# Second input projection of a two-layer encoder: the last third of the tokens is met from unit 6 on

## The reference

```python
x = x + rms_norm(y, g_post)              # end of layer 0, y = output projection
h = rms_norm(x, g_pre)                   # layer 1
q, k, v, gate = jnp.split(h @ w_in, SPLIT_C, axis=-1)   # 1024, 256, 256, 1024 columns
q = rms_norm(q.reshape(B, T, C_HEADS, 64), q_norm)      # per head, then rotary positions; k alike
# attention, then (o * silu(gate)) @ w_out, post-norm, residual
```

## Time and profile before

| | us |
|---|---|
| median of 3 runs | 2140.35 (2137.98 to 2148.28) |
| the profiled execution's own time | 2140.14 |
| its span, first to last instruction | 2138.4 |
| TensorE busy | 2045.5 (96%) |
| VectorE, ScalarE, GpSimd busy | 1291.7, 1125.5, 946.4 |
| mean granted TensorE clock | 0.984 |

### The profile page before, as it was taken

The page is one execution under the profiler, slowest core; times in us unless marked ns, Lnnn a source line. Parts: engine busy times, 40 slices in busy tenths (PEclk is TensorE's granted clock), DMA queues, the critical chain, the costliest instruction groups (busy, mean ns, idle before and its releaser), DMA issues.

```text
span 2138.4 us, 25149 instructions
## 1 busy us (share of the span) xinstructions
PE 2045.5 (96%) x9332; PEld 1629.6 (76%) x9332; DVE 1291.7 (60%) x1928; ACT 1125.5 (53%) x1427; POOL 946.4 (44%) x472
## 2 busy tenths in 40 slices
PE   7999998999999999999997999999999999998995
PEld 6878876788888877767785777888777777775784
DVE  6232135326777766784567777424588778888444
ACT  7142234336666666674355344243677777777331
POOL 1222234335555555565001666432566667666200
PEclk9999999999999999999998999999999999999998
DMA  5133468526665545354335233261333333333434
GB/s 187 42 130 132 148 241 321 148 80 145 133 128 114 110 109 121 86 171 157 93 114 183 83 110 108 89 199 55 76 82 74 70 66 72 80 112 99 158 94 148
DMA packets 167530, 260.29 MB, mean 122 GB/s; under 512 B 75552, under 2 KB 84384, under 8 KB 167408
## 3 DMA queue, kind: packets, MB, share of 16 engines
q1 hardware_dynamic: 167408, 258.68, 42.3%
HBM read 160.72 MB, written 97.91 MB: 121 GB/s over the span
## 4 chain that ended last, share of the span: by engine, by line
PE 82%; DVE 10%; ACT 3%; DMA 3%; issue 2%; POOL 0%; SPq 0%; DVEq 0%; ACTq 0%
PE SA L1813 11%; PE OP L1857 9%; PE SA L473 6%; PE OP L473 5%; PE SM L1739 5%; PE OP L998 5%; PE SA L998 4%; PE OP L1864 4%; PE SA L1912 4%; PE SM L1912 4%; PE OS L473 3%; PE OS L1857 2%; PE OS L998 2%; PE SM L1735 2%; PE OS L1912 2%
## 5 line engine op out<-in xcount | busy, mean ns | idle before, releaser
L2228 POOL TENSOR_TENSOR c_PL<-c_PF,c_PH 128x1024 fp32r<-128x1024 f32 x128 | 308.8, 2417 | 152.2 <-ACT c_PH L1981 81.1
L2228 POOL TENSOR_TENSOR ab_PL<-ab_PF,ab_PH 128x1024 fp32r<-128x1024 f32 (+3 forms) x128 | 266.5, 2085 | 188.9 <-ACT ab_PH L1981 130.8
L1978 ACT ACTIVATE ab_PF<-SA 128x1024 f32<-128x1024 f32 (+3 forms) x160 | 143.6, 897 | 158.0 <-PE SA L1774 83.2
L2056 DVE TENSOR_REDUCE c_MH<-SM 128x1 f32<-128x512 f32 x256 | 171.9, 687 | 75.5 <-PE SM L1739 74.8
L1978 ACT ACTIVATE c_PF<-SA 128x1024 f32<-128x1024 f32 x160 | 164.0, 1025 | 95.3 <-PE SA L1813 95.0
L394 POOL TENSOR_TENSOR e_wl<-e_raw,e_wh 128x1024 fp32r<-128x1024 f32 (+1 forms) x31 | 73.6, 2375 | 218.9 <-ACT e_wh L539 218.9
L1981 ACT ACTIVATE c_PH<-c_PF 128x1024 fp32r<-128x1024 f32 x128 | 135.7, 1061 | 4.1
L1813 PE MATMUL SA<-c_Q,c_KA 128*128 128x512 f32 x320 | 129.6, 405 | 6.4 <-ACT c_PF L1978 6.4
L1739 PE MATMUL SM<-c_KA,c_Q 128*128 128x512 f32 x320 | 127.0, 398 | 4.5 <-DVE c_MH L2056 3.0
L1813 PE MATMUL SA<-c_Q,c_KB 72*128 72x512 f32 x320 | 128.7, 402 | 0.0
L1981 ACT ACTIVATE ab_PH<-ab_PF 128x1024 fp32r<-128x1024 f32 (+3 forms) x128 | 119.6, 935 | 4.0
(11 more groups left out here) (471 smaller groups left out, 5998.3 us busy)
## 6 DMA issues: line engine op xcount, KB each, us to landing
c_Q<-qC_hi SPq DMA_DIRECT2D x32, 384.0 KB, 4.9
e_raw<-in_w_tiles SPq DMA_DIRECT2D x20, 512.0 KB, 4.2
n_raw<-in_w_tiles SPq DMA_DIRECT2D x18, 512.0 KB, 3.8
e_XF<-in_xT SPq DMA_DIRECT2D x12, 512.0 KB, 10.7
silu_gate<-e_ta SPq DMA_DIRECT2D x24, 256.0 KB, 2.0
ab_Q<-qA_hi SPq DMA_DIRECT2D x16, 384.0 KB, 5.3
ab_G<-silu_gate SPq DMA_DIRECT2D x24, 256.0 KB, 3.2
ab_res<-in_xT SPq DMA_DIRECT2D x24, 256.0 KB, 2.9
```

The lines of the kernel that those rows point to most:

```text
L1978: nc.scalar.activation(used(PF[p], h, s), used(SA, h, s), ACT.Exp).then_inc(e_done, 1)
L2056: nc.vector.reduce_max(dst, src, axis=AX_X).then_inc(m_done, 1)
L2228: nc.gpsimd.tensor_tensor(used(PL[p], h, s), used(PF[p], h, s), used(PH[p], h, s).bitcast(F32), ALU.subtract).then_inc(p_lo[0], 1)
```

## The change

`U` is reordered. Units 0 to 3 are gate tiles 0 and 1 in the first two thirds; units 4, 5, 6 are q tile 0 in thirds 2, 0, 1, so that the last third (1) is first met in unit 6; the other q and k tiles follow (to unit 33), the values are units 34 to 39. Gate tiles 0 and 1 in the last third are units 40 and 41, and as their weights are gone by then, both tiles are loaded and split a second time (`W` has 24 entries instead of 22). Gate tiles 2 to 7 keep units 42 to 59. `EARLY = 4` gates come first, in place of 6.

With it: weight tiles 2 and 3 are loaded in period 3 and split in it, by ScalarE at t = 4 and 7 and by GpSimd; units 0 and 1 are evicted in it, ahead of the last two low parts; the seven sums of squares go behind units 1, 2 and 3 in three parts; the sum over partitions and `root` of the last third come with unit 6; the first tables are prepared behind unit 3; units 4, 5 and 6 wait for the stores of gates 0 and 3, 1, 2.

```diff
-        ("values", u, 2, 512) for u in range(4)] + [("x", 12 + t, 8, D) for t in range(6)]
-    U = [(tiles[t], t, c) for c in ORDER for t in range(2)]
-    U += [(tiles[t], t, c) for t in range(2, 12) for c in range(NC)]
+        ("values", u, 2, 512) for u in range(4)] + [("x", 10 + t, 8, D) for t in range(8)]
+    EARLY = 4
+    U = [(tiles[t], t, c) for c in ORDER[0:2] for t in range(2)]
+    U += [(tiles[2], 2, c) for c in ORDER] + [(tiles[t], t, c) for t in range(3, 12) for c in range(NC)]
     U += [(("value", i), V0 + 3, i) for i in range(TT // 2)]
-    U += [(late_gates[t], V0 + 4 + t, c) for t in range(6) for c in range(NC)]
+    U += [(tiles[t], V0 + 4 + t, ORDER[2]) for t in range(2)]
+    U += [(late_gates[t], V0 + 6 + t, c) for t in range(6) for c in range(NC)]
...
-        if (period, t) == (3, 0):
-            load(sp, 2)
+        if (period, t) in ((3, 0), (3, 1)):
+            load(sp, 2 + t)
...
-                if 0 < w < len(W) - 2:
+                if 1 < w < len(W) - 2:
                     load(sp, w + 2)
...
     def gpsimd_ahead(pool):
-        for w in range(2):
+        for w in range(4):
             low_weights(pool, w)
...
-        for g in range(3):
+        for g in range(EARLY):
             gated(g)
-        low_weights(pool, 2)
-        for g in range(3, 6):
-            gated(g)
-        for n in range(6, N):
+        for n in range(EARLY, N):
             for w in splits[n]:
-                low_weights(pool, w)
+                if w > 3:
+                    low_weights(pool, w)
...
             pe.wait_ge(x_sum[c], KT - 1)
+            if c == 2:
+                pe.wait_ge(q_log, 1)
             square_sum(c, ssum[c][:])
...
-            if i < 2:
-                pe.wait_ge(deviation, NC)
+            if i < 3:
+                pe.wait_ge(deviation, i + 1)
...
-            if n in (0, 2, 4):
-                x_square_sum(n // 2)
+            if n in (0, 2, 6):
+                x_square_sum(min(n // 2, 2))
...
+            if t in (4, 7):
+                high_weights(act, 2 + t // 7)
...
-        for g in range(3):
+        for g in range(EARLY):
             sigmoid(g)
-        high_weights(act, 2)
-        root(act, 2)
-        for g in range(3, 6):
-            sigmoid(g)
-        for n in range(6, N):
+        for n in range(EARLY, N):
             for w in splits[n]:
-                high_weights(act, w)
+                if w > 3:
+                    high_weights(act, w)
+            if n == 6:
+                root(act, 2)
...
+        if qk.index(n) < 3:
+            dve.wait_ge(g_stored[s], 32 if s == 0 else 16)
...
             if t == KT + 1:
+                for n in range(2):
+                    evict(dve, n)
                 low_x(dve, 2, 6)
                 low_x(dve, 2, 7)
...
-            evict(n)
-            if n == 2:
-                for k in range(1, KT):
+            if n > 1:
+                evict(dve, n)
+            if n in (1, 2, 3):
+                for k in range(1, KT)[3 * (n - 1):3 * n]:
                     add_square(dve, 2, k)
...
-            if n in (4, 8):
-                prepare(n // 2 - 2)
+            if n in (3, 8):
+                prepare(n // 4)
```

More of the change, by code:

```diff
@@ L1223, in low_x, with evict @@
                                        ).then_inc(x_lo[j], 1)
+    def evict(dve, n):
+        c = U[n][2]
+        if kind[n] == "value":
+            dve.wait_ge(tok_done, 1)
+            dve.wait_ge(hi_done, len(qk) + 2 * (n - v0) + 2)
+            for i in range(2):
+                half, t = slice(i * 256, i * 256 + 256), 2 * (n - v0) + i
+                done = nc.vector.scalar_tensor_tensor(
+                    out=sl[stage_of(n)][:, half].bitcast(F32R), in0=bank(n)[:, half], scalar=rtok[:, t:t + 1],
+                    in1=sh[stage_of(n)][:, half], op0=ALU.mult, op1=ALU.subtract)
+            done.then_inc(acc_read, 1)
+            return
+        dve.wait_ge(mm_done, n + 1)
+        dve.wait_ge(rstd_ready, ORDER.index(c) + 1)
+        if n in gates:
+            g = gates.index(n)
+            if EARLY <= g < EARLY + 3:
+                dve.wait_ge(lo_done, len(qk))
+            wait_count(dve, g_stored[g % 3], 16 * (g // 3))
+            nc.vector.tensor_tensor(ta[g % 3][:], bank(n), rstd[:, cols(c)], ALU.mult).then_inc(acc_read, 1)
+            return
+        s = qk.index(n) % 3
+        if qk.index(n) < 3:
+            dve.wait_ge(g_stored[s], 32 if s == 0 else 16)
+        wait_count(dve, lo_done, qk.index(n) - 2)
+        nc.vector.tensor_tensor(ta[s][:], bank(n), rstd[:, cols(c)], ALU.mult).then_inc(acc_read, 1)
+        dve.wait_ge(acc_read, n + 1)
+        nc.vector.stream_shuffle(tb[s][:], ta[s][:], SWAP16).then_inc(r_swap, 1)
     def vector_ahead(dve, period, t):
@@ L1258, in prepare @@
                                         ALU.mult, ALU.mult).then_inc(tab_done, 1)
[L1260 to L1288, removed]
         def finish(n):
@@ L1307, in low @@
                                     ).then_inc(lo_done, 1)
-        dve.wait_ge(x_sum[1], KT - 1)
         for n in range(N):
```

## The result

The changed kernel takes 2152.41 us (median of 16 runs) where the kernel before, on the same chip, took 2142.2 (median of 16). The ratio is 1.0044, with a 95% interval of 1.0036 to 1.0053: 9.4 us slower. That is a slowing clear of the spread of the runs, and at the edge of the 0.5% that the prediction counts as "no change". The forecast was 2146.7 in a range from 2139.5 to 2153, so the median lies 0.6 us inside the upper end. One of the 16 runs of the changed kernel was slow (3851.26 us at a granted clock of 0.874) and is left out of the ratio; the median of the other 15 is 2152.06. The profiled execution took 2151.08 us (span 2149.3), 10.9 more in span than before. The busy shares, against the earlier trace rows, say nothing of the cause: TensorE is busy 7.2 us longer with as many instructions, as more of its matmuls ran at half clock.

What follows compares the result with a forecast made beforehand. TensorE was taken as the bound, busy 2045.5 of 2138.4 us. Front 0.8 plus reloaded tiles 5.8 gave 6.6 us on the profiled 2140.14, so 2146.7 us, range 2139.5 to 2153.

Steps and rivals of the forecast that it cites:

- The front: Start of the second projection: TensorE restarts 6.2 us later with one more unit (5.44) behind it, 0.8 us slower.
- The two holds: GpSimd's two added splits hold VectorE's last blocks of x: 1.35 us late at the first, 3.5 in all.
- the last low parts: Last two low parts of x on VectorE, waiting for the last store's landing: start at 1154.05, 3.5 us later.
- The pause: TensorE's wait moves behind unit 5, lasts 16 us and ends at 1170.2 through gate 3's chain.
- Tile 17: Reloaded tile wanted at the second unit behind the values; its split comes late, so TensorE waits 3.85 us.
- Tile 18: Next tile behind the values: split at 1418.4, wanted at 1418.6, so hidden by 0.2 us.
- a new wait further on: Sign that the forecast is wrong: TensorE waiting at a later place where the forecast had no wait.
- The clock: Behind the wait for tile 17, TensorE falls to half clock, costing 1.93 us; sum about 5.8 either way.
- Holds that cost nothing: Rival: the added splits fall into VectorE's own waits for residual loads; 3.5 us less, 2143.2 us; chance 0.10.
- Tile 17 in time: Rival: no wait for that tile behind the values, the front's loss alone remains, 2140.9 us; chance 0.10.
- The whole pause gone: Rival: head sum 4 finds its square, all 17.6 us come back, the 5.8 stay, 2128.3 us; chance 0.04.
- The store of gate 3 late: Rival: store in SP's queue lands in 9.2 us, not 2.4; TensorE restarts 6.8 later, 2153.5 us; chance 0.14.

Runs made afterwards that it cites:

- e2: Changed kernel with q and k units moved on by one tile, first tables prepared behind eviction 4: 2147.35 us, ratio 1.0014 to the kernel before.
- e3: Changed kernel with GpSimd's part of the two added weight splits done twice, first into a spare tile: 2152.64 us (one run).
- e4: Changed kernel with VectorE instead of GpSimd computing the low parts of the two added splits: 2156.04 us, ratio 1.0050 to the kernel before.
- e1: Changed kernel with the two reloaded gate tiles put behind gate tiles 2 to 7: 2145.42 us, ratio 1.0010 to the kernel before.
- e8: Changed kernel with the edits of e1 and e2 together: 2143.69 us, ratio 1.0004 to the kernel before.
- e6: e8 with the first gates' evictions and sigmoids taken forward and unit 4 evicted ahead of the additions: 2136.89 us, ratio 0.9977 to the kernel before.
- e7: e6 with VectorE computing the low parts of e4: 2137.19 us, ratio 0.9979 to the kernel before.

## Why the prediction was right, and where it was off

**The front: right, by its own steps.** 0.8 us forecast, 0.7 measured, and the table shows no step off by more than 0.4 us. The two holds were costed from one row of another place, and came out at (2.01 - 0.75) + (2.89 - 0.69) = 3.46 us where I had 3.5; the last low parts start 1155.82 - 1.82 - 1150.55 = 3.45 later than in the earlier trace rows. The pause did move behind unit 5 and grow to 15.9; e2 shows that the wait for gate 3's tile made up the last 4.7 us of it.

**Tile 17: the mechanism right, the size over-estimated.** I took ScalarE's 3.85 us wait for the k stores as it stood in the earlier trace rows; it was 2.40, and TensorE waited 2.39 us, not 3.85. By itself that would have been 1.46 better. It was 2.40 to 2.44 in the traces of all experiments too, so it goes with the new order of units; why, isn't shown. (The 3.85 itself should have been 4.0, as the unit starts at 1401.74.)

**Tile 18: the step that failed.** It is what the prediction gave as a sign of being wrong, a new wait further on where it had none. "Hidden by 0.2" was the difference of two times near 1418, each a sum of terms uncertain by more. Its issue came 1.07 us earlier behind the end of the values than in the earlier trace rows (1401.02 - 1393.38 = 7.64 against 1410.45 - 1401.74 = 8.71), its landing took 1.58 longer, and TensorE wanted it 1.46 earlier because tile 17 was on time: 0.5 + 1.46 - 0.2 is about the 1.94 measured, within 0.2. This also says that the two waits aren't terms of their own: what tile 17 doesn't cost, tile 18 takes, since unit 42 starts when tile 18 is split. Up to there the loss was 1410.66 - 1393.38 - 10.88 = 6.4 us against 5.8 forecast.
Why the landing took 6.08 us is shown in part. SyncE issued the load of tile 19 right behind it (x2 in its row), as tile 17 serves one unit only, and the DMA engines had a share of 0.98 in 1401 to 1405. In the four traces with this pair (the changed kernel, e2, e3, e4) tile 18 landed after 6.1, 6.1, 6.5 and 6.3 us; in the four where its load goes out alone behind the same stores (e1, e8, e6, e7), after 5.1 to 5.2 (here e1's):

```profile
DMA to landing us min/median/max: 5.1/5.1/5.1
```

So about 1 us of the 1.58 goes with the second load, and the rest against the 4.5 of the earlier trace rows is open.

**The clock: right once, and once more than I had.** The fall behind tile 17 was taken at 1.93 us and came at 1.88. That the sum stands either way, since tile 18 is late by as much if the clock doesn't fall, is what e2's trace shows: no fall, and 3.55 us of wait instead of 1.94. I priced no fall behind tile 18, because I had no wait there. This second stretch, 1.94 us, is the term that the sum lacked: 6.4 + 1.94 = 8.3 against 5.8.

**The rivals.** Holds that cost nothing: refuted by the two rows and e3. Tile 17 in time: refuted by its 2.39 us. The whole pause gone: it is longer than before. The store of gate 3 late: it landed in 2.00 us, so nothing of the 6.8 came.

In time, the traces' 10.9 us hold 1.8 from ahead of the change. The runs put the change at 9.4 (ratio) to 10.2 (medians), the steps at 9.0, the forecast at 6.6. That the time still lies inside the range, 0.6 us from its end, is luck in so far as the range wasn't made for the term that was missing. The front was forecast to 0.1 us by this pair of traces.

## What to carry to other kernels

Moving the consumer that starves doesn't remove a pause when another chain, here the reuse of a tile through sigmoid, product and store, ends it at the same place or later; walk that chain first, and take its members (evictions, squares) out from behind bulk work before moving units. With two weight buffers a tile that serves one unit leaves no time for the next load and split, so tiles that are loaded again belong where their neighbours serve several units and no stores crowd the queue. When a step is "hidden by 0.2", price it as open: here the late split of tile 18 came with a stretch at half clock that cost as much as the wait. And a stretch at half clock ahead of a wait that something else ends is no loss of its own, so it must not be added to that wait.

## What the runs showed of the hardware

Waits of TensorE of 2.39 and 1.94 us were each followed by a stretch at half clock (0.50 in 1403 to 1405 and in 1413 to 1415), in which the matmuls took 1.88 and 1.94 us longer. In e2 the first wait, 2.40 us at the same place, was followed by none (1.00 from 1396 to 1400), and the second, 3.55 us, was (0.51 from 1404 to 1406). So such a wait was followed by the lower clock in one trace and not in another.
Stretches at half clock come and go between executions, in stages that all these kernels have alike. Between 84 and 92 us the granted clock was 0.57 in the changed kernel's trace, 1.00 in e8's and 0.79 in the seven others; between 488 and 504 us it was 0.57 in e1's and e6's, 0.68 in e8's and 1.00 in the six others. The time of a run goes with its mean granted clock: of the 23 runs of the kernel before beside e1 to e4, the fastest took 2136.81 us at 0.986 and the slowest 2150.67 at 0.978. A difference of two single traces holds this spread; lay it out by place before you believe it.
A 512 KB weight load took 6.1 to 6.5 us behind 256 KB stores and with another load right behind it (four traces), 5.1 to 5.2 without the other load (four traces), 4.5 in the earlier trace rows, and 3.7 as the median of the earlier trace rows.
VectorE's own subtraction of a 128x1024 tile took 1.23 us, GpSimd's 2.35 to 2.67 us; as GpSimd's held VectorE for up to 2.2 us of it, moving it to VectorE brought nothing that could be measured in the time here.
